# Output product begun inside the attention loop, norms applied after it, half of the gate product beside transposes

## The chip, the cores and the metric

One core of a Trainium2 chip runs the whole kernel in one launch. The time is the device time of one execution in microseconds (us), the median of the runs shown. Engines: PE (TensorE, matrix products), PEld (its weight loads), DVE (VectorE), ACT (ScalarE), POOL (GpSimd), SP (SyncE, which only issues DMAs here). PSUM has 8 banks of 128 x 512 f32.

## What is computed

256 tokens of width 2048 pass through two blocks, batch 1, all f32. The change lies in the first one:

```
h = rms_norm(x);  proj = h @ w_in                # c_q 512, c_kv 256, k_rope 64, x_rec 1024, y_gate 1024
attn = mla(c_q, c_kv, k_rope)                    # 8 heads, q/k of 128+64 (rope), v of 128, causal, blocks of 128
rec  = gelu(y_gate) * scan(a, b(x_rec))          # gated linear recurrence over the 256 tokens, 1024 features
mixed = concat(rms_norm(attn) * g_a, rms_norm(rec) * g_r)
x = x + mixed @ w_out
x = x + peer_ffn(rms_norm(x))                    # 8 heads x top 16 of 16384 experts, rows gathered for every token
```

`peer_ffn` gathers, for each token, 128 rows of `peer_u` (dot products with the token) and 128 rows of `peer_v` (weighted sum), 8 KB each. The second block takes this x and a context of 256 tokens. Its first layer projects both to queries, keys, values and gates, runs a chunked recurrence and an output product; its second layer is a gated spatial mixer. Both are modulated by `cond @ ada_w + ada_b`, where `ada_w` is 96 slabs of 1 MB (48 for each layer), which the kernel reads one by one from its first microsecond on.

## The kernel before

Every engine has one instruction stream written out by hand, with semaphores between them. Activations lie as [feature, token] for products by feature and [token, feature] for products by token. A `Plan` lays down in advance which of the 8 PSUM banks each product takes (in turn: unit number modulo 8), and in which order SP loads weight slabs of 1 MB into a ring of 4 slots. A slot is loaded again when its release semaphore is reached, in the order of the plan: a load that waits holds back all loads behind it.

The stages of the first block in PE's order: `xT` transposes; the input product in parts (`in_q`, `in_kv`, `in_x`); `uq` and `ukv` (queries, keys, values); `gates` (8 small products, 256 wide, for the recurrence); `in_y` (the gate product, 2 chunks of 4 slots); `qkT` (16 units of transposes of q and k, for which PE waits on `qk_ready`, DVE's norms and rotations); the attention loop; the output product `w_out` (4 chunks of 512 features, 4 slots each, L905 and L906); and the query product `pq` of peer_ffn with the scores `psc` per head.

**The attention loop** has 18 steps, software-pipelined over 16 units (8 heads x 2 token blocks): in step s PE does the score of unit s (L873, L874), the transposes of the probabilities of unit s-1 (L882) and the value product of unit s-2 (L889). DVE moves the scores to SBUF with the mask (L1936), takes the maximum (L1940) and the reciprocal of the sum (L1945); ACT does the exponential with the sum (L1297), evacuates the transposed probabilities (L1303) and the output with the reciprocal as factor (L1311). In step 11 the squares of the recurrent part are summed over features by 8 products with a matrix of ones (`rec_ss`, L897); ACT and DVE make a factor per token, and DVE applies it with the gain to `MIX[0:8]` (L1958).

**After the loop** DVE sums the squares of the attention output, makes the norm and scales; PE transposes it in 16 tiles (`att_turn`, before slot 1 of `w_out` chunk 0); ACT and DVE evacuate it with the gain to `MIX[8:16]`. Then `w_out` goes on. DVE adds each of its 8 units to x (L1987). `f_turn(c)` transposes chunk c of the new x for the query product.

**Slabs of ada_w.** DVE takes the dot products of each slab with one or two condition rows (L1744, `ada_dots`); `ADA_FIRST` says how many slabs at which point of DVE's stream, 48 in all before the gathers begin: among them 8 ahead of the norms and rotations (key `ukv`), 21 in `w_out`, and 3 just ahead of the first top-16 search (key `pq`). POOL issues these 48 loads. The other 48 come through SP's ring in the second block (`ADA_AT`: how many behind each slot of a chunk).

**The recurrence.** POOL multiplies the input gate by the conv output (L619, wait `ix_ready`); DVE makes the factors (L1903, L1904, L1907), scans (L1910) and then evacuates the rope part of `qkT`; POOL multiplies the scan by the gelu of the gate (L623) and squares it (L625).

**Scores.** ACT evacuates the query of head h (L1363), then the scores of head h-1 (L1355). DVE's search of head 0 (L2015 on) waits for the scores of head 0, and POOL's first gather (L646) for that search.

## Time and profile before

| | us |
|---|---|
| median of 3 runs (lowest, highest) | 2701.57 (2695.4, 2702.32) |
| profiled execution, its own time | 2707.62 |
| span of that execution | 2705.8 |
| PE busy | 1948.8 (72%) |
| DVE busy | 1973.8 (73%) |
| ACT busy | 567.8 (21%) |
| POOL busy | 1051.9 (39%) |
| attention loop, first score to first w_out product | 235.24 to 287.08 |
| w_out until PE turns to the query product | 287.08 to 402.77 |
| first gather issued | 442.37 |
| second block's first transpose | 1812.93 |

The busy shares are averages over stages with different limits. The span has four parts: the dense first block to about 403 us, the query product and the start of the gathers, the gathers to 1812 us, and the second block.

### The profile page before, as it was taken

The numbers are of one execution on the slowest core, as the hardware profiler recorded it, in microseconds if no ns is written. First come the engines' busy times: TensorE is split into PE (matmuls) and PEld (weight loads), VectorE is DVE, ScalarE is ACT, GpSimd is POOL, SyncE is SP. The second block draws the span as 40 slices with busy tenths as digits, with TensorE's granted clock in tenths as the row PEclk, the third lists the DMA queues.
The fourth block names the chain that finished last, engine by engine and source line by source line (L and its number), as shares of the span: only waits on it lengthen the run. The fifth ranks groups of instructions, "written<-read, shape, count | busy, mean of one in ns | idle before, by whom it ended". The sixth has DMA issues, their size and how long they took to land.

```text
span 2705.8 us, 20658 instructions
## 1 busy us (share of the span) xinstructions
PE 1948.8 (72%) x7632; PEld 1336.7 (49%) x7632; DVE 1973.8 (73%) x2459; ACT 567.8 (21%) x829; POOL 1051.9 (39%) x648
## 2 busy tenths in 40 slices
PE   8999999799003777777777000019999999899997
PEld 5876448647001222222222000019888887788885
DVE  6885886886997667544444999998855689777666
ACT  3043110100000000010000000013443343544343
POOL 0011002363687555545545788850065650000000
PEclk9997999899556999999999555559999999999998
DMA  9671787999999999999999999977853459677552
GB/s 374 251 292 64 293 333 282 404 371 421 416 422 422 421 421 422 422 422 421 422 422 422 421 422 422 421 315 283 323 190 125 170 180 359 262 295 286 207 200 100
DMA packets 123508, 887.60 MB, mean 328 GB/s; under 512 B 13840, under 2 KB 14352, under 8 KB 16528
## 3 DMA queue, kind: packets, MB, share of 16 engines
q0 software_dynamic: 80640, 587.24, 52.6%
q1 hardware_dynamic: 39024, 276.58, 27.5%
q10 hardware_dynamic: 3744, 22.47, 2.1%
q8 instruction: 61, 1.00, 0.1%
q14 instruction: 39, 0.32, 0.0%
HBM read 884.13 MB, written 2.10 MB: 328 GB/s over the span
## 4 chain that ended last, share of the span: by engine, by line
PE 38%; DMA 26%; POOL 16%; DVE 15%; issue 4%; ACT 2%; ACTq 0%; DVEq 0%; SPq 0%
PE psum L778 22%; DMA W<-in_peer_v,W 15%; POOL W L646 9%; POOL early_rows L646 6%; PE psum L710 6%; DMA W<-in_peer_u,W 5%; PE psum L975 3%; PE psum L734 2%; DVE split L1758 2%; DMA early_rows<-in_peer_v,W 2%; DMA early_rows<-in_peer_u,W 1%; DVE early_rows L2085 1%; DVE W L2085 1%; PE psum L926 1%; DMA ring<-in_w_even 1%
## 5 line engine op out<-in xcount | busy, mean ns | idle before, releaser
L778 PE MATMUL psum<-split,hi 128*128 128x512 f32 x1664 | 516.0, 391 | 5.4 <-DVE split L1758 4.0
L2085 DVE CUSTOM_DVE_ANT_0 W<-W,XN 128x2048 f32<-128x2048 f32 x147 | 334.2, 2292 | 207.4 <-DMA W<-in_peer_u,W 206.6
L1209 ACT ACTIVATE split<-ring 128x1024 fp32r<-128x1024 f32 x272 | 283.0, 1057 | 405.0 <-PE psum L778 299.1
L975 PE MATMUL psum<-early_rows,HT 128*128 128x512 f32 x408 | 189.1, 607 | 246.9 <-ACT HT L1415 181.0
L975 PE MATMUL psum<-W,HT 128*128 128x512 f32 x616 | 284.1, 604 | 99.2 <-DMA W<-in_peer_v,W 99.2
L2085 DVE CUSTOM_DVE_ANT_0 early_rows<-early_rows,XN 128x2048 f32<-128x2048 f32 x109 | 247.7, 2291 | 140.8 <-DMA early_rows<-in_peer_u,W 139.5
L778 PEld LDWEIGHTS psum<-split,hi 128*128 128x128 f32 x1664 | 312.2, 188 | 72.1 <-issue 6.1
L1758 DVE TENSOR_TENSOR split<-ring,split 128x1024 fp32r<-128x1024 f32 x208 | 250.3, 1227 | 130.2 <-ACT split L1209 129.2
L646 POOL DMA_INDIRECT W<-in_peer_v,W x153 | 280.5, 1833 | 163.3 <-PE psum L975 129.9
L646 POOL DMA_INDIRECT W<-in_peer_u,W x147 | 207.2, 1410 | 143.6 <-DVE W L2085 58.2
L975 PEld LDWEIGHTS psum<-early_rows,HT 128*128 128x128 f32 x408 | 74.1, 191 | 361.5 <-issue 260.9
L975 PEld LDWEIGHTS psum<-W,HT 128*128 128x128 f32 x616 | 111.5, 190 | 271.7 <-ACT HT L1415 148.8
L672 POOL TENSOR_TENSOR split<-ring,split 128x1024 fp32r<-128x1024 f32 x64 | 159.8, 2519 | 213.8 <-ACT split L1209 213.8
L988 PE MATMUL psum<-cst,X 128*128 128x128 f32 x32 | 5.1, 333 | 322.0 <-DVE X L2169 322.0
L646 POOL DMA_INDIRECT early_rows<-in_peer_v,W x103 | 184.0, 1786 | 116.8 <-PE psum L975 97.4
L646 POOL DMA_INDIRECT early_rows<-in_peer_u,W x109 | 157.6, 1446 | 121.7 <-DVE W L2085 93.7
L2163 DVE SCALAR_TENSOR_TENSOR X<-W,X 128x2048 f32<-128x2048 f32 x75 | 176.4, 2352 | 10.5 <-DMA W<-in_peer_v,W 1.2
L1415 ACT ACTIVATE HT<-cst,W 128x128 f32<-128x128 f32 x128 | 51.1, 401 | 566.6 <-PE psum L975 566.6
L734 PE MATMUL psum<-HT,ring 128*128 128x256 f32 x768 | 166.5, 379 | 0.0
L988 PEld LDWEIGHTS psum<-cst,X 128*128 128x128 f32 x32 | 4.8, 179 | 322.9 <-DVE X L2169 322.9
L734 PEld LDWEIGHTS psum<-HT,ring 128*128 128x128 f32 x768 | 145.8, 190 | 20.3 <-issue 0.4
L778 PE MATMUL psum<-split,lo_odd 128*128 128x512 f32 x384 | 149.5, 389 | 0.0
(366 smaller groups left out, 3126.9 us busy)
## 6 DMA issues: line engine op xcount, KB each, us to landing
ring<-in_ada SPq DMA_DIRECT2D x48, 1024.0 KB, 6.1
ring<-in_odd SPq DMA_DIRECT2D x48, 1024.0 KB, 5.2
XN<-in_ada POOLq DMA_DIRECT2D x21, 1024.0 KB, 8.3
early_rows<-in_ada POOLq DMA_DIRECT2D x16, 1024.0 KB, 8.1
ring<-in_w_out SPq DMA_DIRECT2D x16, 1024.0 KB, 7.6
ring<-in_pq SPq DMA_DIRECT2D x16, 1024.0 KB, 9.3
ring<-in_c_v SPq DMA_DIRECT2D x16, 1024.0 KB, 7.7
ring<-in_c_k SPq DMA_DIRECT2D x16, 1024.0 KB, 7.9
```

The costliest lines, as they stand in the source:

```text
L646: nc.gpsimd.indirect_dma_start(row, None, t["peer_" + table], bass.IndirectOffsetOnAxis(ap=EIDX[:, c:c + 1], axis=0),).then_inc(full, 16)
L672: nc.gpsimd.tensor_tensor(split[:, to + 1024:to + 2048], ring[:, at:at + 1024], split[:, to:to + 1024], ALU.subtract).then_inc(sem("lo_poo ...
L710: m = nc.tensor.matmul(o[tt][:, 0:width], lhs[:, k, tt * P:(tt + 1) * P], sl[:, kk * width:(kk + 1) * width], start=(k == 0), stop=(k == s ...
L734: m = nc.tensor.matmul(o[a][:, S * b:S * b + S], sl[:, kk * 512 + m4 * P:kk * 512 + m4 * P + P], rhs[:, k, :], start=(k == 0 and b == 0), ...
L778: m = nc.tensor.matmul(dst, lhs, rhs, start=(k == 0 and b == 0 and not (features and i % 2)), stop=(k == KD - 1 and b == 2 and not (featur ...
L926: m = nc.tensor.matmul(o[:, S * b:S * b + S], sl[:, k * P:(k + 1) * P], ht[:, k, :], start=(k == 0 and b == 0), stop=(k == KD - 1 and b == 1))
L975: m = nc.tensor.matmul(o[c], DIAG[j % DIAGS], row[:, 512 * c:512 * c + 512], start=(j == 0), stop=(j == P - 1))
L1209: A(split[:, 2048 * (n % PIECES):2048 * (n % PIECES) + 1024], ring[:, at:at + 1024], ACT.Copy)\
L1415: A(DIAG[j % DIAGS], IDENT, ACT.Copy, scale=PACT[:, j:j + 1]).then_inc(sem("diag_ready"), 1)
L1758: TT_(split[:, to + 1024:to + 2048], ring[:, at:at + 1024], split[:, to:to + 1024], ALU.subtract)\
L2085: V.tensor_tensor_reduce(out=row, in0=row, in1=xn3[:, tt, :], scale=1.0, scalar=0.0, op0=ALU.mult, op1=ALU.add, accum_out=PACT[:, c:c + 1])\
L2163: STT(x3[:, 1, :], row, PACT[:, P + j:P + j + 1], x3[:, 1, :], ALU.mult, ALU.add)\
```

## The change

- `in_y` chunk 1 is cut into 16 parts of 4 products. 8 parts follow chunk 0; one part follows the transposes of each head in `qkT`. Its gelu comes after `qkT` on ACT. The two banks that it fills are taken out of the turn meanwhile.
- `w_out` chunk 0 has separate accumulators for the recurrent features (`w_out_r`, slots 0 and 1) and the attention features (`w_out_a`, slots 2 and 3), and so have the other chunks. Slot 0 of chunk 0 is multiplied in steps 1 and 2 of the attention loop and slot 1 in steps 8 to 15. Slots 2 and 3 follow the loop.
- The norms of both groups become factors per token, applied when DVE adds the units of `w_out` to x: 16 additions with a factor (`out_add`) in place of 8 plain ones. The sums of squares come from 32 products with one column of ones (`mix_squares`), between slots 2 and 3 of chunk 0; `rec_ss`, `att_turn`, `ao_squares` and the scaling go.
- The value product is by feature: V is the stationary operand, its result is the transposed output, which DVE writes with the gain to MIX; ACT takes its square. The reciprocal of the softmax sum goes into a diagonal matrix (`DIAG_P`, one DVE instruction per unit), and the transposes of the probabilities become products with it. The loop has 19 steps, with lags 2 and 3 for 1 and 2.
- The squares of q are taken by ACT (16 instructions behind the evacuations of `ukv`) and no more by DVE. The product of input gate and conv output, and that of scan and gelu (in two halves), go from POOL to DVE. DVE scans a head's 256 columns and evacuates a head of `qkT` in turn.
- Slabs: of the 8 ahead of the norms 1 stays, 3 go between the two token blocks, 4 before the scans. The 3 ahead of the first search go into SP's ring, one each in `l_q` chunk 0, `l_v` chunk 0 and `l_v` chunk 1.
- ACT evacuates the scores of head h right behind the query of head h.

The diff, cut:

```diff
 
-ADA_FIRST = {"in": 8, "in_x0": 4, "in_x1": 2, "conv": 2, "ukv": 8, "w_out0": 5, "w_out1": 5, "w_out2": 5, "w_out3": 6,
-             "pq": 3}
+ADA_FIRST = {"in": 8, "in_x0": 4, "in_x1": 2, "conv": 2, "rope0": 1, "rope1": 3, "rope2": 4,
...
 ADA_AT = {}
-ADA_AT["l_q", 0] = (0, 0, 0, 1)
-for _step in (("l_q", 1), ("l_k", 0), ("l_k", 1), ("l_v", 0), ("l_v", 1)):
+ADA_AT["l_q", 0] = (0, 0, 1, 1)
+for _step in (("l_q", 1), ("l_k", 0), ("l_k", 1)):
     ADA_AT[_step] = (1, 1, 1, 0)
+ADA_AT["l_v", 0] = ADA_AT["l_v", 1] = (1, 1, 1, 1)
 ADA_AT["l_g", 0] = (4,)
...
+    y_late, out_early = [("in_y", 2), ("in_y", 3)], [("w_out_r", 0), ("w_out_r", 1)]
+    p.keep(y_late)
     p.units("qkT", 16)
-    for step in range(2 * NH + 2):
-        for name, lag in (("score", 0), ("probT", 1), ("pv", 2)):
+    for key in out_early:
+        p.place(key)
+    p.keep(out_early)
+    p.give_back(y_late)
+    for step in range(2 * NH + 3):
+        for name, lag in (("score", 0), ("probT", 2), ("pv", 3)):
             if 0 <= step - lag < 2 * NH:
-                p.unit[name, step - lag] = len(p.unit)
-        if step == REC_STEP:
-            p.units("rec_ss", 1)
...
+            def y_part(k):
+
+                s, kk = k // 4, k % 4
+                n = plan.slot["in_y", 1, s]
+                if kk == 0:
+                    slot_of("in_y", 1, s)
+                sl = ring[:, 2048 * (n % RING):2048 * (n % RING) + 2048]
+                for m4 in range(4):
+                    a, b = m4 // 2, m4 % 2
+                    m = nc.tensor.matmul(y_units[a][:, S * b:S * b + S], sl[:, kk * 512 + m4 * P:kk * 512 + m4 * P + P],
+                                         ht[:, k, :], start=(k == 0 and b == 0), stop=(k == KD - 1 and b == 1))
+                    if k == KD - 1 and b == 1:
+                        close(m, ("in_y", 2 + a))
+                if kk == 3 and s < 3:
+                    m.then_inc(sem("slot_used"), 1)
+
+            for k in range(8):
+                y_part(k)
             pe.wait_ge(sem("qk_ready"), TT)
             for h in range(NH):
                 for i, (n, qs, ks) in enumerate(((DN, lambda tt: qr4[:, tt, h, 0:DN], lambda tt: kv4[:, tt, h, 0:DN]),
...
                     close(m, ("qkT", 2 * h + i))
-            pe.wait_ge(sem("qkT_act"), NH)
-            pe.wait_ge(sem("qkT_dve"), NH)
...
+                    pe.wait_ge(sem("mix_rec"), 4)
+                    slot_of("w_out", 0, 0)
+                    out_part(0, 0, range(0, 2))
+                if step == 2:
+                    out_part(0, 0, range(2, 4))
+                if 8 <= step < 16:
+                    n = step - 8
+                    if n == 0:
+                        pe.wait_ge(sem("mix_rec"), 8)
+                        slot_of("w_out", 0, 1)
+                    out_part(0, 1, [n // 2], [n % 2])
+                i = step - 2
                 if 0 <= i < 2 * NH:
-                    pe.wait_ge(sem("prob_ready"), i + 1)
+                    pe.wait_ge(sem("att_diag"), i + 1)
                     o = open_unit(("probT", i))
                     for kt in range(i % 2 + 1):
-                        m = nc.tensor.transpose(o[:, kt * P:(kt + 1) * P], PR[:, i % 2, kt * P:(kt + 1) * P], IDENT)
+                        m = nc.tensor.matmul(o[:, kt * P:(kt + 1) * P], PR[:, i % 2, kt * P:(kt + 1) * P],
+                                             DIAG_P[:, i % 2, :], start=True, stop=True)
...
                 if 0 <= i < 2 * NH:
                     pe.wait_ge(sem("probT_ready"), i + 1)
                     o = open_unit(("pv", i))
                     for kt in range(i % 2 + 1):
-                        m = nc.tensor.matmul(o[:, 0:P], PT[:, i % 2, kt * P:(kt + 1) * P], kv4[:, kt, i // 2, DN:2 * DN],
+                        m = nc.tensor.matmul(o[:, 0:P], kv4[:, kt, i // 2, DN:2 * DN], PT[:, i % 2, kt * P:(kt + 1) * P],
                                              start=(kt == 0), stop=(kt == i % 2))
...
-                transposes("attT", 8, lambda k, tt: AO[:, tt, k * P:(k + 1) * P])
-
-            pe.wait_ge(sem("mix_rec"), 8)
-            token_chunk("w_out", 0, MIX, before={1: att_turn, 2: lambda: pe.wait_ge(sem("mix_att"), 4)})
+
+
+            def mix_squares():
+                pe.wait_ge(sem("rec_sq"), 1)
+                pe.wait_ge(sem("att_sq"), 2 * NH)
+                o = open_unit(("ss", 0))
+                sq3 = GA.rearrange("p (j s) -> p j s", j=8)
+                for half, sq in enumerate((SQA, sq3)):
+                    for tt in range(TT):
+                        at = 2 * half + tt
+                        for j in range(8):
+                            m = nc.tensor.matmul(o[:, at:at + 1], sq[:, j, tt * P:(tt + 1) * P], ONES[:, 0:1],
+                                                 start=(at == 0 and j == 0), stop=(at == 3 and j == 7))
+                close(m, ("ss", 0))
+
             def f_turn(c):
                 def turn():
...
 
+            out_open("w_out_a", 0)
+            slot_of("w_out", 0, 2)
+            for kk in range(4):
+                pe.wait_ge(sem("mix_att"), 2 * kk + 2)
+                out_part(0, 2, [kk])
+            mix_squares()
...
                 give(m, ("ukv", i))
+
+                if i % 2:
+                    tt = i // 4
+                    if tt:
+                        act.wait_ge(sem("q_ss"), NH)
+                    for h in range(2 * (i % 4) - 2, 2 * (i % 4) + 2):
+                        A(SQQ[:, h, :], qr4[:, tt, h, :], ACT.Square, accum_out=st(120 + 8 * tt + h))\
...
-            gelus(1)
-            for i in (2, 3):
-                gave(act, ("in_y", i))
+            gave(act, ("in_y", 1))
             act.sem_inc(sem("yg_ready"), 1)
 
+
+            used = plan.release[plan.slot["in_y", 1, 1]][0][1]
+            act.wait_ge(sem("slot_used"), used)
             for h in range(NH):
                 wait_unit(act, ("qkT", 2 * h))
...
+            def att_square(i):
                 wait_unit(act, ("pv", i))
-                m = A(AO[:, i % 2, (i // 2) * P:(i // 2 + 1) * P], bank(("pv", i))[:, 0:P], ACT.Copy, scale=st(80 + i))
-                give(m, ("pv", i))
...
-                if h:
-                    scores_evac(h - 1)
-            scores_evac(PH - 1)
+                scores_evac(h)
...
 
-            ada_dots(ADA_FIRST["ukv"])
+            ada_dots(ADA_FIRST["rope0"])
...
                 dve.sem_inc(sem("qk_ready"), 1)
-
+                if tt == 0:
+                    ada_dots(ADA_FIRST["rope1"])
...
             dve.wait_ge(sem("tanh_ready"), 8)
             dve.wait_ge(sem("decay_sq"), 1)
             seq(STT(TMP, TMP, 1.0, RR, ALU.add, ALU.mult))
             TS(TMP, TMP, 1.0e-30, None, ALU.max).then_inc(sem("mult_sq"), 1)
+            ada_dots(ADA_FIRST["rope2"])
             dve.wait_ge(sem("mult_ready"), 1)
-            dve.wait_ge(sem("ix_ready"), 1)
             seq(TT_(TMP, TMP, II, ALU.mult))
...
+            def rec_product(half):
+                a = slice(1024 * half, 1024 * half + 1024)
+                dve.wait_ge(sem("yg_ready"), half + 1)
+                seq(TT_(II[:, a], XC[:, a], YG[:, a], ALU.mult))
+                dve.sem_inc(sem("rec_out"), 1)
+
+            def rec_gain(half):
+                for j in range(4 * half, 4 * half + 4):
+                    TS(MIX[:, j, :], II[:, S * j:S * j + S], column("rec_g", j), None, ALU.mult).then_inc(sem("mix_rec"), 1)
+
+            for h in range(NH):
+                a = slice(S * h, S * h + S)
                 seq(V.tensor_tensor_scan(XC[:, a], GA[:, a], TMP[:, a], 0.0, ALU.mult, ALU.add))
...
+                if step == 1:
+                    rec_product(1)
+                    rec_gain(1)
+
...
+                    TS(DIAG_P[:, i % 2, :], IDENT, st(80 + i), None, ALU.mult).then_inc(sem("att_diag"), 1)
...
+                    m = TS(MIX[:, 8 + h, tt * P:(tt + 1) * P], bank(("pv", i))[:, 0:P], column("attn_g", h), None, ALU.mult)
...
+            def out_add(name, c, at):
+
+                for tt in range(TT):
+                    i = 2 * c + tt
+                    wait_unit(dve, (name, i))
+                    dst = x3[:, tt, 512 * c:512 * c + 512]
+                    m = STT(dst, bank((name, i)), st(at + tt), dst, ALU.mult, ALU.add)
+                    give(m, (name, i))
+                    gave(dve, (name, i))
+                    if name == "w_out_a":
...
+            for c in range(4):
+                ada_dots(2)
+                if c == 0:
+                    wait_unit(dve, ("ss", 0))
+                    m = V.tensor_copy(st(16, 4), bank(("ss", 0))[:, 0:4])
+                    give(m, ("ss", 0))
+                    gave(dve, ("ss", 0))
+                    rstd(st(12, 4), st(16, 4), ATT, EPS)
+                out_add("w_out_r", c, 14)
+                ada_dots(ADA_FIRST[f"w_out{c}"] - 2)
+                if c:
+                    evac_T("fT", ht, scale=lambda k: column("ffn_g", k), units=(2 * c - 1,))
+                out_add("w_out_a", c, 12)
```

## Rows read from the trace of the kernel before

**Rows 1.** One line of the page's costliest groups: busy, mean ns | idle before, releaser

```profile
L2085 DVE CUSTOM_DVE_ANT_0 W<-W,XN 128x2048 f32<-128x2048 f32 x147 | 334.2, 2292 | 207.4 <-DMA W<-in_peer_u,W 206.6
```

**Rows 2.** Windows, one core: window, length, busy time (instructions) per engine, PEclk, DMA share, GB/s

```profile
245.00:250.00 5.00, 5.00 (x17) 3.25 (x17) 1.68 (x7) 1.98 (x8) 0.00 (x0) 0.50 0.00 0
272.00:275.00 3.00, 3.00 (x18) 2.10 (x18) 2.24 (x10) 1.79 (x5) 0.00 (x0) 1.00 0.00 0
431.00:443.00 12.00, 12.00 (x62) 10.66 (x61) 8.01 (x35) 1.44 (x3) 0.63 (x1) 1.00 0.41 129
1000.00:1200.00 200.00, 148.59 (x323) 58.20 (x322) 116.39 (x163) 17.65 (x42) 102.55 (x80) 0.99 1.01 421
```

**Rows 3.** PE timeline before attention: start, duration, line, instructions [idle before <-releaser]

```profile
164.35 55.42 PE L734 MATMUL psum<-HT,ring 128*128 128x256 f32 x256
228.05 1.05 PE L863 MATMUL psum<-cst,W 128*64 128x128 f32 x6 [4.35 <-DVE XN L1916]
```

**Rows 4.** PE timeline in the attention loop: pair starts at either clock, and w_out's start

```profile
244.75 0.63 PE L873 MATMUL psum<-HT 128*128 128x128 f32 x2
...
250.21 0.63 PE L873 MATMUL psum<-HT 128*128 128x128 f32 x2
...
271.48 0.38 PE L873 MATMUL psum<-HT 128*128 128x128 f32 x2
...
274.47 0.39 PE L873 MATMUL psum<-HT 128*128 128x128 f32 x2
...
287.08 8.48 PE L710 MATMUL psum<-ring,W 128*128 128x512 f32 x16
```

**Rows 5.** PE timeline of the output product and the first query head

```profile
339.22 27.63 PE L710 MATMUL psum<-ring,W 128*128 128x512 f32 x64
...
407.95 1.04 PE L914 MATMUL psum<-cst,X 128*128 128x128 f32 x8
408.82 10.53 PE L926 MATMUL psum<-HT,ring 128*128 128x256 f32 x48
419.19 1.05 PE L937 MATMUL psum<-W 128*128 128x128 f32 x8
```

**Rows 6.** The chain that ended last: start, length, what

```profile
153.22 9.97 DMA XN<-in_ada
```

**Rows 7.** DVE timeline of the norms and rotations

```profile
176.49 6.07 DVE L1883 TENSOR_TENSOR W<-W 128x1536 f32<-128x1536 f32 x1
...
197.04 1.76 DVE L1883 TENSOR_TENSOR W<-W 128x1536 f32<-128x1536 f32 x1
...
213.36 2.29 DVE L1903 SCALAR_TENSOR_TENSOR W<-W 128x2048 f32<-128x2048 f32 x1 [0.22 <-DVE W L1898]
```

**Rows 8.** DVE groups of the attention stretch, and three rows of its timeline after

```profile
L1936 DVE SCALAR_TENSOR_TENSOR W<-psum,stat,cst 128x128 f32<-128x128 f32 (+1 forms) x16 | 6.7, 417 | 25.7 <-PE psum L874 25.6
L1940 DVE TENSOR_REDUCE stat<-W 128x1 f32<-128x128 f32 (+1 forms) x16 | 5.6, 353 | 0.6
...
298.99 2.35 DVE L1744 CUSTOM_DVE_ANT_0 early_rows<-early_rows,col 128x2048 f32<-128x2048 f32 x1 [0.37 <-DVE W L1971]
...
402.97 0.69 DVE L1987 TENSOR_TENSOR X<-psum,X 128x512 f32<-128x512 f32 x1 [0.17 <-PE psum L710]
...
433.65 0.49 DVE L2015 MAX8 W<-W 128x8 f32<-128x128 f32 x2 [5.03 <-ACT W L1355]
```

**Rows 9.** ACT timeline: a value product's evacuation, and the first scores

```profile
156.78 0.60 ACT L1251 ACTIVATE X<-psum 128x512 f32<-128x512 f32 x1 [1.98 <-PE psum L710]
...
417.66 0.60 ACT L1363 ACTIVATE W<-psum 128x512 f32<-128x512 f32 x1 [8.09 <-PE psum L926]
...
433.14 0.84 ACT L1355 ACTIVATE W<-psum,stat 128x256 f32<-128x256 f32 x2 [0.18 <-ACT W L1363]
```

**Rows 10.** SP's queue of DMA issues in the value chunks of the second block

```profile
1915.06 0.33 SPq L584 DMA_DIRECT2D ring<-in_c_v  x1
...
1957.26 0.33 SPq L584 DMA_DIRECT2D ring<-in_c_v  x1
```

238 lines of the change are left out of this document (118 added, 120 removed).

## The prediction

> **What bounds the kernel now.** I read the page's slices first, then the chain that ended last, then the windows and timelines of the stretch that the change touches. From the first gather to the second block the kernel is bound by DMA: in the middle of the gathers the DMA share is 1.01 and the rate 421 GB/s [rows 2] (the window of 200 us), and DVE's dot products of u rows sat 206.6 us waiting for rows [rows 1]. Nothing in the change alters the bytes gathered. So the first part counts only by when it lets the gathers start, and by how well the DMA engines are used until then. The first part is bound by PE for most of its length: `in_y` runs 55.42 us without a break [rows 3], the output product 27.63 us for every 64 instructions [rows 5]. Between these two lies the stretch that the change aims at: `qkT`, where PE waits 4.35 us for DVE [rows 3], and the attention loop, where a pair of steps takes 5.46 us at the lower clock (244.75 to 250.21) and 2.99 us at the full one (271.48 to 274.47) [rows 4]. The granted clock there is 0.50 although PE is busy 5.0 of 5 us [rows 2]. DVE has much room in it: its mask instructions waited 25.6 us for scores [rows 8].
>
> **PE's new path to the output product.** `in_y` still costs 55.4 us from 164.35 [rows 3], now with the transposes of `qkT` inside: 64 of 0.11 us (eight take 0.87 us from start to start, 407.95 to 408.82 [rows 5]), 7.0 us. If nothing stalls, the loop starts at 164.4 + 55.4 + 7.0 = 226.8.
>
> Three waits could break that. (1) PE waits for `qk_ready` at 164.4 + 55.4 x 3/4 = 205.9. DVE begins its norms when ACT has evacuated `ukv`, 158.3 (the last pair starts at 156.78 [rows 9]), and no more at 176.5 behind 8 slabs, one of which landed 9.97 us after its issue [rows 6]. One token block took 213.36 - 197.04 = 16.3 us [rows 7]; without q's square and its reduction, 1.76 us each, it takes 12.8. Two blocks and three slabs of 2 dots or one, here single ones of 2.35 us [rows 8], end at 158.3 + 25.6 + 7.1 = 191: 15 us of room. ACT's 16 squares are narrower than the 256-wide score copies (0.42 us each [rows 9]) but also read an accumulator; at 0.42 to 0.6 us, four fit in the 1.98 us that ACT idles before each pair of `ukv` [rows 9], so they cost nothing, and 2 us if late, inside the same room. (2) The first rope copy of `qkT`: DVE does two 2048-wide products at 2.29 us [rows 7], one scaling of 1.2, four dots (9.4) and one more product: 191 + 17.5 = 208.5, plus what the last slab is late. Its place comes free only after the first of those four dots (about 199) and a load lands 5 to 10 us later, so DVE starts its scans between 208.5 and 213.5. PE can run three heads ahead (6 banks), until about 213.6. So the cost is 0 to 4 us, taken as 1. (3) In the loop's step 1 PE waits for `mix_rec` 4, about 1 us after the last copy, with the probabilities of all units queued behind it: 1 us, up to 5 if (2) is late.
>
> **The loop.** Eight pairs at 3.0 us [rows 4] are 24.0. The 24 transposes of probabilities become f32 products with twice the instructions: 24 x 0.11 = 2.6. Half of `w_out` chunk 0, 32 instructions at 27.63/64 = 0.43 us [rows 5], is 13.8; it only moves, from behind the loop. DVE per step: mask 0.42, maximum 0.35 [rows 8], reciprocal, diagonal and evacuation, each no larger than these: some 1.8 us with handshakes, so a pair takes 3.6 where PE alone would take 3.3. That costs 0.5 us in the unfilled steps; the filled ones (5.1 us a pair on PE) hide it. The last value products are a chain of three engines: 1.5 us. With the waits (2) and (3) the loop ends at L = 226.8 + 24.0 + 2.6 + 13.8 + 0.5 + 1.5 + 2 = 271. In the old kernel `w_out` began at 287.08 [rows 4] with nothing done.
>
> **The output product.** PE: second half of chunk 0 13.8; `mix_squares`, 64 instructions of one column. No row shows a product of one column with full weights; the transposes load as much: 64 x 0.11 = 7.0 us, bounded by 0 and by twice that at the lower clock. Then three chunks 82.9, three `f_turn` 2.6, and the 24 instructions of the query product ahead of `f_turn(3)`, 5.2. `f_turn(3)` starts at L + 111.5 = 382.5, against 407.95 [rows 5]: 25.5 us earlier. DVE beside it: 37 dots at 2.35 [rows 8] are 87; 16 additions of 0.69 [rows 8] and a handshake 12.5; norms and evacuations 6; and it begins only when x is reloaded, 5 to 10 us after L. That ends at L + 112: DVE is as late as PE. Its time is an upper one, since the dots overlap a little, but here the gain could lose 5 us. The old attention norm, its 16 transposes and `rec_ss` are gone from both; that is in the sum already, as what no longer stands between.
>
> **The first search.** In the old kernel the scores of head 0 were computed at 419.19 [rows 5] and evacuated at 433.14, behind the query of head 1 [rows 9]; the search started at 433.65 after 5.03 us of idleness [rows 8]. Now it can start about 1.9 us after 419.19, as that row shifts: 12 us sooner still. The three dots that go, 7 us of DVE, lay in this idle time and are worth nothing beyond it. But the gathers are bound by DMA bytes: 12 us of earlier issue is worth only what the DMA engines idled there, 1 - 0.41 of 12 us = 7 (window 431 to 443 [rows 2]), less the time until the first rows flow. I take 5, with bounds 2 and 12.
>
> **The second block.** Three slabs more go through SP's ring. In the value chunks 14 loads took 1957.26 - 1915.06 = 42.2 us, 3.25 each [rows 10], and the chain there runs through the ring. The one in `l_v` chunk 0 costs 3.25. The one in `l_q` chunk 0 lies beside products of PE, the last in `l_v` chunk 1 behind that chunk's own loads: 0 to 3.25 each. I take 5 us, bounds 2 and 10. Behind SP's waits stand only ring loads.
>
> **POOL and ACT queues.** POOL loses two 2048-wide products. One ran beside DVE's square of q, which took 6.07 us against 1.76 for its twin [rows 7]; that is gone. The one left falls beside DVE's first steps of the loop and can slow them by 4 us, under PE's 6.9 us of filler. The slab loads behind POOL's wait for `rec_out` come at 231, as before.
>
> **Sum.** 25.5 + 5 - 5 = 25.5 us. The profiled execution took 2707.6 (span 2705.8); it would take 2682. It stands 6 us over the median 2701.6, so on the median's scale 2676.
>
> **The clock.** The loop's 43 us are reckoned at the full clock, and this is the largest bet. For it: PE comes from 62 us of products without a long pause; the 3 us at 272 to 275 held 1.00; and the gathers' products, busy 148.6 of 200 us, held 0.99 [rows 2]. Against it: the old loop stayed at 0.50 for 30 us while recorded as busy throughout [rows 2, 4]. The Trainium skill, "TensorE: Matmul & The Clock Gate", Part 1, says that sustained activity lifts the throttle; by that alone the old loop would have warmed, and the row says it did not. The same page, Part 4 (PE-mode transpose), says transposes do not count as activity like other products; that would make the new loop, where the probabilities' transposes became products, warmer than the old. No row here separates the two.
>
> **Rivals.**
> A, the forecast: 2676, its own range 2665 to 2688; chance 0.53.
> B, part of the loop is cold: the unfilled steps (3 to 7, 16 to 18, four pairs) go at 5.46 + 0.6 in place of 3.6: +10 us, 2686; chance 0.15.
> C, slower: PE pauses at the rope copies (wait 2), the clock falls, and as in the old loop does not return before `w_out`. Then the loop is 8 x 5.46 + 5.1 + 27.5 = 76 us in place of 43, +33; with 4 us of wait and 4 us for a cold `w_out` start and `mix_squares`, 2676 + 41 = 2717. It decides once the loop costs over 34 us more than reckoned. Chance 0.05.
> D, DVE's slabs bind the output product and the ring's turn costs its upper bound: 5 + 5 + 2 for the evacuations: 2688; chance 0.12. For it: DVE's sum equals PE's.
> E, more is gained: the search's lead counts in full (12 in place of 5) because the later DMA gaps close too, and the moved slabs cost 2: 2666; chance 0.10.
> F, the change doesn't do what it says: the gathers' end is held by something other than their start, and only the first block is shorter: 2700; against it, the DMA share of 1.01 from there on. Chance 0.05.
>
> **How the numbers follow.** Predicted 2676. The range 2659 to 2699 leaves out C and a part of F. A measurement of this kernel can tell about 0.3%, 8 us, from no change: faster means below 2693.5. Of A, B, D and E nearly all lies below: 0.87. Within: F and the edge of B and D, 0.08. Slower: C, 0.05.
>
> **What would show it.** No idle of PE over 2 us between `in_y` and the loop's start at 227; granted clock 1.00 in the loop; its pairs 3.6 us unfilled and 5.1 filled; `w_out`'s second half at 271; 64 instructions of `mix_squares` in 7 us; `f_turn(3)` at 382; first gather at 405, that is 37 us earlier; the second block's first transpose some 30 us earlier; its value chunks 5 us longer. I am wrong if the loop's pairs take 5.5 us, if DVE is still in its slabs when PE has waited for `f_turn(3)`, or if the gathers end less than 20 us earlier.

## The result, and the profile after

The changed kernel took 2688.7 us (median of 5 runs, 2683.7 to 2694.9), the kernel before 2702.3 us in the same comparison (2695.4 to 2708.8): a ratio of 0.9949, with a 95% interval of 0.9933 to 0.9965. It is faster (the whole interval lies below 1), by 13.6 us where I had forecast 25.5. On the scale of the profiled executions the sum had said 2682 against 2707.6; the profiled execution after took 2689.7 (span 2687.8), a gain of 17.9.

| step, us from the start | before | forecast | after |
|---|---|---|---|
| attention loop starts | 235.24 | 226.8 | 226.61 |
| loop ends, rest of w_out starts | 287.08 | 271 | 274.87 |
| f_turn(3) | 407.95 | 382.5 | 393.07 |
| first gather | 442.37 | 405 | 414.70 |
| second block's first transpose | 1812.93 | about 1782 | 1789.72 |
| span | 2705.8 | 2680 | 2687.8 |

The timeline of PE in the changed kernel (start, duration, line, instructions; in brackets the idle time before, with what ended it), where [rows 3 to 5] stood before:

```profile
205.79 0.38 PE L916 MATMUL psum<-cst,W 128*128 128x128 f32 x2
...
226.61 0.38 PE L952 MATMUL psum<-W,HT 128*128 128x128 f32 x2
...
242.62 0.39 PE L952 MATMUL psum<-W,HT 128*128 128x128 f32 x2
...
247.83 0.39 PE L952 MATMUL psum<-W,HT 128*128 128x128 f32 x2
...
253.57 0.39 PE L952 MATMUL psum<-W,HT 128*128 128x128 f32 x2
...
258.78 0.39 PE L952 MATMUL psum<-W,HT 128*128 128x128 f32 x2
...
274.87 7.71 PE L930 MATMUL psum<-ring,W 128*128 128x512 f32 x16
282.42 9.96 PE L995 MATMUL psum<-cst,W 128*128 128x1 f32 x64
292.23 29.93 PE L930 MATMUL psum<-ring,W 128*128 128x512 f32 x64
...
351.21 27.63 PE L930 MATMUL psum<-ring,W 128*128 128x512 f32 x64
...
391.24 1.99 PE L1035 MATMUL psum<-HT,ring 128*128 128x256 f32 x8 [1.20 <-ACTq L1278]
393.07 1.04 PE L1007 MATMUL psum<-cst,X 128*128 128x128 f32 x8
```

`qkT` starts at 205.79 with the parts of `in_y` between its transposes, nothing waits, and the loop starts where the sum had it. In the loop a pair of steps takes 5.2 us whether it has no filler (242.62 to 247.83) or has it (253.57 to 258.78): this unfilled pair, the last before the filler, is 1.6 us longer than forecast (the one ahead of it, from 238.54, took 4.08). Behind the loop the same 16 instructions take 7.71 us that take 7.03 at the full clock, `mix_squares` takes 9.96, and the 64 instructions after it take 29.93 against 27.63. The clock has its own view (windows; the fields are those of [rows 2]; PEclk is the third from the right):

```profile
250.00:260.00 10.00, 9.93 (x47) 6.32 (x46) 5.87 (x20) 3.75 (x15) 0.00 (x0) 1.00 0.01 2
...
273.00:275.00 2.00, 1.91 (x9) 1.61 (x9) 0.35 (x1) 0.66 (x2) 0.00 (x0) 0.50 1.04 438
278.00:282.00 4.00, 4.00 (x11) 1.72 (x10) 0.00 (x0) 0.00 (x0) 0.00 (x0) 1.00 0.90 340
282.00:285.00 3.00, 3.00 (x26) 2.76 (x25) 0.00 (x0) 0.00 (x0) 0.00 (x0) 1.00 1.01 423
285.00:288.00 3.00, 3.00 (x23) 3.00 (x22) 2.63 (x3) 0.00 (x0) 0.00 (x0) 0.74 1.02 431
288.00:291.00 3.00, 3.00 (x16) 3.00 (x16) 3.00 (x3) 0.00 (x0) 0.53 (x1) 0.50 0.91 385
...
403.00:416.00 13.00, 13.00 (x66) 11.54 (x65) 8.01 (x35) 1.22 (x3) 1.00 (x1) 1.00 0.65 230
```

The loop runs at 1.00, which was the largest bet (the old one at 0.50 [rows 2]). At its end, where the last value products wait for other engines, the clock falls to 0.50, recovers, and falls a second time inside `mix_squares`, some 4 us after its start, and stays low behind it. The waits of the loop, and those behind it up to the gathers (engine, tile and line that waited <- what it waited for: us in all, times, longest):

```profile
ACT W L1417 <- DVE stat L2054: 17.0, 12, 1.6
DVE W L2071 <- ACT W L1430: 10.1, 12, 1.0
...
DVE early_rows L1850 <- DMA X<-in_x: 9.6, 1, 9.6
```

In the loop VectorE waits 12 times for the square (L1430) that ScalarE takes of a value product, before it may evacuate the same product (L2071); ScalarE's exponential (L1417) in turn waits for VectorE's maximum (L2054), and the square stands behind it in ScalarE's queue. That is a ring of two queues, not a bound of PE. Behind the loop VectorE waits 9.6 us for x to be reloaded, and then works through the slabs until the last addition; PE waits 1.20 us at 391.24 for the copy of a tile that it had turned at 378.68. VectorE's last addition, ScalarE behind it, and VectorE's search:

```profile
387.82 1.65 DVE L2085 SCALAR_TENSOR_TENSOR X<-psum,stat,X 128x512 f32<-128x512 f32 x2
...
388.66 0.63 ACT L1450 ACTIVATE W<-X 128x512 f32<-128x512 f32 x1 [22.60 <-DVEq L2089]
...
390.18 0.96 ACT L1273 ACTIVATE HT<-psum,col 128x256 f32<-128x256 f32 x2
...
405.98 0.49 DVE L2127 MAX8 W<-W 128x8 f32<-128x128 f32 x2 [5.80 <-ACT W L1463]
```

```profile
414.70 1.00 POOL L680 DMA_INDIRECT W<-in_peer_u,W  x1 [40.06 <-DVEq L2179]
```

The copy (L1273) doesn't read what VectorE's last addition writes. It stands in ScalarE's queue behind the squares of the new x (L1450), and those waited 22.60 us for that addition. So VectorE's lateness reaches PE through the order of ScalarE's queue, 1.8 us after the addition has ended (389.47 to 391.24), and then PE has 8 more instructions of the query product to do before `f_turn(3)`.

The search starts at 405.98 (433.65 before [rows 8]) and the first gather is issued at 414.70, 27.7 us earlier than before: 14.9 from `f_turn(3)`, 12.8 from the earlier evacuation of the scores. The second block starts 23.2 us earlier and the span ends 18.0 earlier.

### The profile page after: what moved, and what is told of

The parts are those of the page before. It is cut to its first block, busy times and chain, and to the rows that moved or that the text cites. A ratio compares the mean times of both kernels' runs of the same rounds, so it can differ in the third digit from the quotient of the medians.

```text
span 2687.8 us, 20829 instructions
## 1 busy us (share of the span) xinstructions
PE 1945.1 (72%) x7688; PEld 1336.5 (50%) x7688; DVE 1978.4 (74%) x2460; ACT 567.1 (21%) x854; POOL 1042.9 (39%) x643
## 4 chain that ended last, share of the span: by engine, by line
PE 39%; DMA 25%; POOL 17%; DVE 13%; issue 4%; ACT 2%; ACTq 0%; DVEq 0%; SPq 0%
PE psum L812 22%; DMA W<-in_peer_v,W 15%; POOL W L680 10%; POOL early_rows L680 7%; DMA W<-in_peer_u,W 5%; PE psum L768 3%; PE psum L744 3%; PE psum L1084 3%; PE psum L930 2%; DMA early_rows<-in_peer_u,W 2%; DVE split L1864 2%; DMA ring<-in_w_even 1%; PE psum L900 1%; DVE early_rows L2197 1%; DVE W L2197 1%
## 5 line engine op out<-in xcount | busy, mean ns | idle before, releaser
L768 PE MATMUL psum<-HT,ring 128*128 128x256 f32 x640 | 138.9, 379 | 0.0
L768 PEld LDWEIGHTS psum<-HT,ring 128*128 128x128 f32 x640 | 121.4, 190 | 17.0 <-issue 0.4
```

The lines of the kernel that those rows point to most:

```text
L768: m = nc.tensor.matmul(o[a][:, S * b:S * b + S], sl[:, kk * 512 + m4 * P:kk * 512 + m4 * P + P], rhs[:, k, :], start=(k == 0 and b == 0), ...
```

## The experiments

Each kernel is the changed one with the edit shown. Milestones are of the profiled execution of each, medians and ratios (to the kernel before, timed beside it) of 5 to 12 runs; f_turn(3) is where PE turns the last tiles of x1, x2T the second block's first transpose.

| kernel | f_turn(3) | first gather | x2T | median us | ratio [95%] |
|---|---|---|---|---|---|
| changed kernel | 393.07 | 414.70 | 1789.72 | 2688.7 | 0.9949 [0.9933, 0.9965] |
| x_evac4 | 393.28 | 414.92 | 1789.55 | 2687.0 | 0.9952 [0.9940, 0.9964] |
| x_spread | 396.56 | 418.43 | 1792.45 | 2691.7 | 0.9969 [0.9957, 0.9981] |
| x_slabs | 393.40 | 422.83 | 1795.16 | 2690.5 | 0.9967 [0.9955, 0.9980] |
| x_lag | 392.89 | 427.40 | 1797.08 | 2697.2 | 0.9987 [0.9976, 0.9998] |
| x_waitx | 391.74 | 413.37 | 1787.81 | 2685.6 | 0.9942 [0.9923, 0.9960] |
| x_front | 387.58 | 410.49 | 1785.88 | 2684.2 | 0.9942 [0.9921, 0.9962] |
| x_ywhole | 404.95 | 426.59 | 1801.80 | 2700.6 | 0.9997 [0.9984, 1.0009] |
| x_nofill | 399.21 | 420.85 | 1795.99 | 2694.2 | 0.9978 [0.9964, 0.9992] |
| x_best | 396.52 | 418.08 | 1791.85 | 2682.1 | 0.9928 [0.9907, 0.9950] |
| x_evacx | 386.61 | 408.24 | 1783.71 | 2682.6 | 0.9932 [0.9914, 0.9949] |
| x_ptrans | 393.64 | 415.28 | 1789.96 | 2687.3 (1 run) | none |
| x_final | 383.64 | 405.20 | 1779.31 | 2678.9 | 0.9923 [0.9906, 0.9941] |

The intervals are 3 to 6 us wide on each side, so differences of 2 or 3 us between kernels are read from the milestones, which agree within 0.5 us at f_turn(3) where nothing ahead of them differs (x_lag, x_slabs and the changed kernel: 392.89 to 393.40) and within 0.9 us at the loop's start (226.48 to 227.31, all but x_ywhole).

**x_evac4: the ring of two queues in the loop.** VectorE's evacuation of a value product moves one step back in its own queue.

```diff
-            for step in range(2 * NH + 3):
+            for step in range(2 * NH + 4):
...
-                i = step - 3
+                i = step - 4
                 if 0 <= i < 2 * NH:
                     h, tt = i // 2, i % 2
                     dve.wait_ge(sem("att_sq"), i + 1)
```

> The changed kernel, with VectorE's evacuation of a value product into MIX one step later in its queue (lag 4 in place of 3), so that its next mask no longer stands behind ScalarE's square of the same unit. Theory (the attention loop is a chain VectorE mask, maximum, ScalarE exponential, copy, square, VectorE evacuation, mask again, 2.6 us a step, whatever TensorE does): the unfilled pairs (from 242.6) fall from 5.2 us to about 4, the filled ones stay at 5.1 by TensorE, the loop is 4 to 6 us shorter, total 2684. Rival 1 (TensorE bounds the loop, it is recorded as busy): pairs stay 5.2, total 2689, no gain. Rival 2 (the loop gets shorter but VectorE's slabs behind it, done at 389 us, hold the output product): loop 5 us shorter, f_turn(3) at most 3 us earlier, total 2687.

PE, x_evac4:

```profile
242.69 0.39 PE L952 MATMUL psum<-W,HT 128*128 128x128 f32 x2
...
246.44 0.39 PE L952 MATMUL psum<-W,HT 128*128 128x128 f32 x2
...
270.25 7.03 PE L930 MATMUL psum<-ring,W 128*128 128x512 f32 x16
277.12 10.63 PE L995 MATMUL psum<-cst,W 128*128 128x1 f32 x64
287.61 29.23 PE L930 MATMUL psum<-ring,W 128*128 128x512 f32 x64
...
389.90 3.54 PE L1035 MATMUL psum<-HT,ring 128*128 128x256 f32 x8 [5.18 <-ACTq L1278]
```

An unfilled pair takes 3.75 us (242.69 to 246.44), near the forecast's 3.6, and the rest of w_out starts at 270.25 in place of 274.87: the ring had cost 4.6 us, some 1.5 in the unfilled pair, 0.8 in the four filled ones (5.14 us each here) and 2.4 behind the last score, where the clock fell in the changed kernel and did not here. Nothing of it arrived. PE waits 5.18 us ahead of f_turn(3), and the 8 instructions behind that pause take 3.54 us where 1.99 do without it. So rival 2 of the expectation holds, with even less gain than it gave: the loop was bound by the chain of VectorE and ScalarE, and the stretch behind it by VectorE, whose lateness ScalarE's queue passes on. VectorE's last addition ends at 388.13, 1.3 us earlier than in the changed kernel, and f_turn(3) starts 5.2 us after that end (3.6 in the changed kernel): ScalarE's squares of x and the copy behind them come in between, then the 8 instructions at the low clock. With the copy ahead of the squares in ScalarE's queue f_turn(3) could have followed at about 388 (an estimate from these rows); no run tests it. VectorE waits 12.9 us for x in place of 9.6, until 284.03 (285.37 in the changed kernel): the reload starts 4.6 us earlier and lands 1.3 earlier.

**x_spread: what mix_squares costs, and the clock.** The 32 products leave their place behind the loop; the plan gives `ss` a bank of its own for the loop.

```diff
+                if 4 <= step < 8:
...
+                    for n in range(4 * (step - 4), 4 * (step - 4) + 4):
+                        square_sum(1, n // 8, n % 8)
+                i = step - 4
+                if 0 <= i < 2 * NH:
+                    pe.wait_ge(sem("att_sq"), i + 1)
+                    square_sum(0, i % 2, i // 2)
...
-            mix_squares()
```

> The changed kernel, with the 32 products of mix_squares taken from their place between the parts of w_out and spread over the attention loop (recurrent ones in steps 4 to 7, one attention one per step from step 4). Theory (at its place mix_squares cost 9.96 us and let the clock fall for some 3 us more of the products behind it; in the loop TensorE has room because the loop runs at the pace of other engines): loop 0 to 3 us longer, f_turn(3) 9 to 13 us earlier (about 382), total 2679. Rival 1 (VectorE's slabs beside the output product, done at about 389, bind next): f_turn(3) only 4 us earlier, total 2685. Rival 2 (the loop is bound by TensorE, so the products cost there what they cost behind it): loop 10 us longer, only the clock's 3 us are won, total 2686.

PE, x_spread:

```profile
277.26 7.11 PE L930 MATMUL psum<-ring,W 128*128 128x512 f32 x16
...
284.36 27.71 PE L930 MATMUL psum<-ring,W 128*128 128x512 f32 x64
...
392.98 3.78 PE L1044 MATMUL psum<-HT,ring 128*128 128x256 f32 x8 [11.10 <-ACTq L1287]
```

The loop is 2.4 us longer, the 64 instructions behind it take 27.71 us, near the full clock's 27.63, and PE gets so far ahead of VectorE that it waits 11.10 us. f_turn(3) came 3.5 us later: 1.7 because VectorE's last addition did (389.56 for 387.82), and 1.8 because the 8 instructions behind the pause took 3.78 us for 1.99. The theory was right about PE and wrong about the total; rival 1, VectorE, bound, and harder than it said, since 5.4 us lie here too between the end of its last addition (391.21) and f_turn(3). The 7.0 us of the forecast for `mix_squares` were the price at the full clock: 34 of its 64 instructions took 3.85 us in x_final, 0.11 each. The other 3.0 us of its 9.96 are the clock, with 2.3 behind it and 0.7 ahead of it, from the loop's end: 6 us in all. In this kernel the same products, one to five in a step, did not let the clock fall.

**x_waitx and x_front: what binds behind the loop.** VectorE waited for x ahead of two slabs that don't read x.

```diff
-            for tt in range(TT):
-                dve.wait_ge(sem(f"x_loaded{tt}"), 32)
...
                 ada_dots(2)
                 if c == 0:
+                    for tt in range(TT):
+                        dve.wait_ge(sem(f"x_loaded{tt}"), 32)
                     wait_unit(dve, ("ss", 0))
```

x_waitx is this alone, x_front this with the edits of x_evac4 and x_spread.

> The changed kernel, with VectorE's wait for the reload of x (9.6 us of idleness at 285.37) moved behind the first two slabs of w_out, which don't need x. Theory (VectorE and TensorE were equally late at f_turn(3), so relief of VectorE alone is worth only the 1.2 us that TensorE waited there): VectorE reaches the last addition 9 us earlier, f_turn(3) 1.2 us earlier (391.9), total 2687.5. Rival (VectorE's lateness held more than that wait shows, such as the query product's evacuation behind it): f_turn(3) 4 us or more earlier, total 2684.

> Three edits together: the evacuation one step later, mix_squares spread over the attention loop, and VectorE's wait for x behind the first two slabs. Alone the first two moved f_turn(3) by +0.2 and +3.5 us, with TensorE waiting there 5.2 and 11.1 us. Theory (TensorE's gain was real and was lost to VectorE's slabs, which start with the wait for x): f_turn(3) at 380 to 384 in place of 393.07, first gather as much earlier, total 2679. Rival 1 (the slabs' loads, at 8.5 us each through places that VectorE frees, set VectorE's pace, not the wait for x): f_turn(3) no earlier than 389, total 2685. Rival 2 (an earlier search finds the DMA engines taken by reloads, so that the gathers end no earlier than x_lag's price of 0.6 us per us says): f_turn(3) at 382, total 2682.

Alone it moved f_turn(3) by 1.3 us, the wait of PE at 391.24, and the total by 3 us by the medians, within their error. VectorE was hardly relieved: in place of 9.6 us for x it now waits 7.3 us for the sums of `mix_squares`, and its last addition comes 1.9 us earlier (385.90). PE sets the pace from there. The forecast's two sums (L + 111.5 and L + 112) had the two engines equally late; measured without its wait PE would have been at f_turn(3) at about 391.9, 2.4 us behind the end of VectorE's last addition. In x_front the three edits together gave 5.5 us at f_turn(3), 387.58, between theory (380 to 384) and rival 1. The timeline of VectorE shows why, and PE's that it still waits:

```profile
277.54 2.35 DVE L1859 CUSTOM_DVE_ANT_0 early_rows<-early_rows,col 128x2048 f32<-128x2048 f32 x1 [0.26 <-DVE W L2080]
...
380.58 1.65 DVE L2091 SCALAR_TENSOR_TENSOR X<-psum,stat,X 128x512 f32<-128x512 f32 x2
```

```profile
384.00 3.78 PE L1044 MATMUL psum<-HT,ring 128*128 128x256 f32 x8 [4.76 <-ACTq L1287]
```

From 277.54 to the end of the last addition at 382.2 VectorE has no pause over 0.6 us: 104.7 us of work from the end of the loop, which itself ended late (276.56, x_evac4's at 270.25): with the ring open PE bounds the filled pairs, and the squares in them count. The other part is ScalarE's order: its copy began at 382.94, behind the squares of x, PE went on at 384.00 at the low clock, and f_turn(3) came 5.4 us after VectorE's last addition had ended. Without that delay it would have stood at about 382, inside the theory's range (again an estimate, not tested).

**x_nofill: is the filler free?** The second half of w_out's recurrent part of chunk 0 goes behind the loop.

```diff
-                if 8 <= step < 16:
-                    n = step - 8
-                    if n == 0:
-                        pe.wait_ge(sem("mix_rec"), 8)
-                        slot_of("w_out", 0, 1)
-                    out_part(0, 1, [n // 2], [n % 2])
...
+            pe.wait_ge(sem("mix_rec"), 8)
+            slot_of("w_out", 0, 1)
+            out_part(0, 1)
             out_open("w_out_a", 0)
```

> The changed kernel, with the second half of w_out's recurrent part of chunk 0 (16 instructions, 6.9 us) taken out of steps 8 to 15 of the attention loop and put behind it. Theory (the loop is bound by the chain through VectorE and ScalarE): pairs stay 5.2 us, the loop ends where it did, the 6.9 us come on top, f_turn(3) 5.7 us later (TensorE's wait of 1.2 goes), total 2694. Rival 1 (TensorE bounds the filled pairs): the loop is 5 to 7 us shorter, total 2689. Rival 2 (the filler is what keeps the clock up): granted clock 0.50 from step 8, loop 3 us longer or more, total 2699.

```profile
275.39 14.79 PE L930 MATMUL psum<-ring,W 128*128 128x512 f32 x32
```

The loop ended at 275.39 without the filler and at 274.87 with it, having started 0.65 later, its pairs at 5.2 us throughout; f_turn(3) came 6.1 us later. The theory holds: the loop's length is the chain's, and 6.9 us of products in steps 8 to 15 cost next to nothing there (48.26 us of loop with them, 48.13 without). The clock stayed at 1.00 without them.

**x_ywhole: is the interleaving of in_y free?** All parts of in_y ahead of qkT.

```diff
-            for k in range(8):
+            for k in range(16):
                 y_part(k)
...
-                y_part(8 + h)
```

> The changed kernel, with all 16 parts of in_y ahead of qkT, so that its 64 transposes stand in one run, as in the kernel before. Theory (the interleaving hides VectorE's eight rope copies and scans, 1.74 us a head): VectorE reaches its first mask some 9 us later (236 in place of 227.45), the loop ends 7 to 9 us later, clock 1.00 throughout because TensorE makes no pause of over 2 us, total 2697. Rival 1 (64 transposes in one run let the clock fall, as it was 0.59 behind them in the kernel before): granted clock 0.50 in the loop, pairs over 5.5 us, total over 2710. Rival 2 (TensorE is three heads ahead, so only 3 us are lost): total 2692.

f_turn(3) came 11.9 us later, and the total is that of the kernel before (ratio 0.9997). VectorE reached its first mask at 236.23 in place of 227.45, 8.8 us later, as the theory said; but the clock fell too, against the theory. Windows of x_ywhole at the loop's start and once more in its unfilled steps:

```profile
229.00:232.00 3.00, 0.47 (x4) 0.38 (x2) 2.64 (x5) 2.84 (x4) 0.00 (x0) 0.93 0.00 0
232.00:235.00 3.00, 2.79 (x7) 1.62 (x7) 2.72 (x6) 0.81 (x1) 0.00 (x0) 0.50 0.00 0
235.00:238.00 3.00, 2.34 (x4) 0.84 (x3) 2.78 (x10) 0.71 (x3) 0.00 (x0) 0.50 0.00 0
238.00:241.00 3.00, 3.00 (x5) 1.21 (x4) 2.85 (x2) 0.38 (x2) 1.98 (x1) 0.50 0.00 0
...
253.00:256.00 3.00, 1.88 (x11) 1.37 (x10) 1.77 (x6) 1.15 (x4) 0.00 (x0) 0.91 0.00 0
256.00:259.00 3.00, 3.00 (x9) 1.70 (x8) 1.77 (x7) 0.93 (x4) 0.00 (x0) 0.50 0.00 0
```

PE was busy 0.47 of 3 us there, waiting for rope copies, and went on at 0.50 until about 242. The clock was at 1.00 behind the transposes (226 to 229) and fell after PE's pauses, so rival 1's cause, the run of transposes, isn't what the windows show. It fell again at about 255.5, behind a pause of 1.06 us, and was low for some 7 us; the same pause at the same place left the changed kernel at 1.00. With the interleaving taken out, the whole gain of 13.6 us but 1.7 is gone, in two ways: VectorE's scans and copies no longer lie beside products (8.8 us), and PE pauses and loses the clock (the other 3). The costs of single parts taken out don't add up to 13.6 (11.9 here, 8.5 in x_lag, 5.5 in x_nofill, by the medians), since the change also has parts that cost time.

**x_ptrans: products or transposes.** The probabilities are turned by the identity, and the division by the softmax sums is missing from the output.

```diff
-                        m = nc.tensor.matmul(o[:, kt * P:(kt + 1) * P], PR[:, i % 2, kt * P:(kt + 1) * P],
-                                             DIAG_P[:, i % 2, :], start=True, stop=True)
+                        m = nc.tensor.transpose(o[:, kt * P:(kt + 1) * P], PR[:, i % 2, kt * P:(kt + 1) * P], IDENT)
```

> The changed kernel, with the 24 transposes of probabilities as transposes by the identity again; the division by the softmax sums is left out with it. Theory (the loop's full clock comes from the work that surrounds it without a pause, not from what form the transposes have; the loop's length comes from the chain through VectorE and ScalarE): granted clock 1.00 to 270, loop end at 274 to 275, total within 3 us of 2689. Rival (transposes lift the clock less than products): granted clock below 0.9 in the unfilled steps, loop 3 us longer or more.

```profile
244.00:247.00 3.00, 1.89 (x8) 1.24 (x9) 1.75 (x7) 1.15 (x4) 0.00 (x0) 0.89 0.00 0
247.00:250.00 3.00, 3.00 (x11) 1.90 (x10) 1.95 (x8) 1.25 (x5) 0.00 (x0) 0.50 0.00 0
...
253.00:256.00 3.00, 3.00 (x14) 1.69 (x13) 1.61 (x5) 0.67 (x3) 0.00 (x0) 0.97 0.00 0
```

At the end of the first unfilled steps, where x_nofill and the changed kernel held 1.00, the clock fell to 0.50 for some 7 us, and the loop ended at 275.85, 1.0 us later (it had started 0.5 later): the clock went as the rival said, the length as the theory. The length doesn't show what the low clock cost, since the filled pairs behind it took 4.8 us here and 5.2 in the changed kernel. The Trainium skill, "TensorE: Matmul & The Clock Gate", Part 4 (PE-mode transpose), says that transposes don't count as busy time as products do; this run agrees with it. It is one execution, with the form the number of instructions changed (24 transposes for 48), and x_ywhole's clock fell in the same steps with the transposes as products. So it is in line with the rule and does not show it.

**x_lag: the lead of the first search.**

```diff
                 act.sem_inc(sem("pq_ready"), 1)
-                scores_evac(h)
+                if h:
+                    scores_evac(h - 1)
+            scores_evac(PH - 1)
```

> The changed kernel, with the score evacuation of head h put back behind the query evacuation of head h + 1 in ScalarE's queue, as in the kernel before. Theory (the lead of 12.8 us of the first gather is worth 8 us at the end of the gathers, because the DMA engines are about 0.65 busy in that time): first gather 12 to 13 us later, x2T about 8 us later, total 2697. Rival 1 (my forecast's price): 5 us, total 2694. Rival 2 (the lead counts in full, the gathers only shift): 12.8 us, total 2701.

The first gather came 12.7 us later and x2T 7.4 us later: 0.58 us per us of lead. The theory's number holds, its reason does not: the share of 0.65 is that of 403 to 416 in the changed kernel, almost all of it ahead of the first gather at 414.70. In x_lag the DMA share was 0.34 in 414 to 427, the stretch that the lead had filled with gathers; 0.66 of 12.7 us idle there are 8.4 us, an estimate near the 7.4.

**x_slabs: the three slabs back ahead of the search.**

```diff
+             "pq": 3}
...
+ADA_PLACE += [("early", "cond")[_n % 2] for _n in range(3)]
...
-ADA_AT["l_q", 0] = (0, 0, 1, 1)
...
+ADA_AT["l_q", 0] = (0, 0, 0, 1)
...
-ADA_AT["l_v", 0] = ADA_AT["l_v", 1] = (1, 1, 1, 1)
...
             dve.wait_ge(sem("fn_ready"), 2 * TT)
+            ada_dots(ADA_FIRST["pq"])
```

> The changed kernel, with the three ada slabs put back from the second block to their old place ahead of the first search (their dot products, 3 of 2.35 us on VectorE, and their loads). Theory (the slabs cost 5.2 us in the value chunks of the second block, and ahead of the search VectorE idles 5.8 us, which hides all but 1.3 us of the 7.05): first gather 1.3 us later, second block 5 us shorter, total 2685. Rival 1 (the slabs land late, behind the reload of x, g and the query weights, and hold the search): first gather 5 us or more later, total 2689, nothing won. Rival 2 (the second block's 5 us come from elsewhere, such as the added dot products in VectorE's queue): no gain in the block, total 2690.

```profile
411.84 2.35 DVE L1853 CUSTOM_DVE_ANT_0 early_rows<-early_rows,col 128x2048 f32<-128x2048 f32 x1 [6.66 <-DMA early_rows<-in_ada]
...
422.83 1.01 POOL L683 DMA_INDIRECT W<-in_peer_u,W  x1 [19.10 <-DVEq L2183]
```

Two of the three dot products fitted into VectorE's idle time; the third waited 6.66 us for its load. The gather came 8.1 us later and x2T 5.4 later; at the transposes of x3, behind the even layer of the second block, the two kernels stood within 0.1 us (2296.81 and 2296.88), so the slabs cost 5.4 us in the second block. The theory had the block right and the search wrong, rival 1 was the case; in the total nothing is won or lost.

**x_best, x_evacx and x_final: both engines at once.** x_evacx has the edits of x_evac4 and x_waitx. x_best has them too, with the squares in steps 4 to 7 and 16 to 18, one dot product ahead of the search, and the recurrent squares added on GpSimd first:

```diff
-             "w_out0": 5, "w_out1": 5, "w_out2": 5, "w_out3": 6}
+             "w_out0": 5, "w_out1": 5, "w_out2": 5, "w_out3": 5,
+             "pq": 1}
...
             nc.gpsimd.tensor_tensor(GA, II, II, ALU.mult).then_inc(sem("rec_sq"), 1)
+            for n, half in enumerate((1024, 512, 256)):
+                pool.wait_ge(sem("rec_sq"), n + 1)
+                nc.gpsimd.tensor_tensor(GA[:, 0:half], GA[:, 0:half], GA[:, half:2 * half], ALU.add)\
+                    .then_inc(sem("rec_sq"), 1)
```

> Five edits: VectorE's evacuation one step later; its wait for x behind the first two slabs; GpSimd adds the recurrent squares over their eight blocks, so that TensorE needs 2 products for them in place of 16; the attention squares' products stand in steps 4 to 7 and 16 to 18 of the loop, where TensorE has room, and not in the filled steps; and one single slab's dot product goes behind the norm of x1, ahead of the search, where VectorE idles 5.8 us. Theory (TensorE and VectorE have to be relieved together): loop ends at 270 to 272, no low clock behind it, f_turn(3) at 378 to 381 against 393.07, search start as much earlier, total 2677. Rival 1 (VectorE's slabs still bind: its 36 dot products and additions take 102 us from the loop's end): f_turn(3) at 384, total 2682. Rival 2 (an earlier search gains only 0.6 us per us): total 2681 with f_turn(3) at 380.

> Two edits: the evacuation one step later and the wait for x behind two slabs; mix_squares stays at its place. Theory (mix_squares costs there its 10.6 us and 1.6 us of low clock behind it, spread in steps 8 to 15 of a loop that TensorE now bounds it cost 6.3): loop ends at 270.3 as in x_evac4, f_turn(3) at 386 to 387, total 2683, the same as x_front. Rival (VectorE binds both): f_turn(3) at 381, no later than x_front's slabs allow, total 2679.

x_evacx did what it should: f_turn(3) at 386.61, no wait of PE, 2682.6 us. x_best's profiled execution shows what the forecast had as rival C. VectorE, then PE, then the clock, x_best:

```profile
230.84 8.30 DVE L2040 TENSOR_SCALAR W<-W,col 128x256 f32<-128x256 f32 x4
```

```profile
239.62 0.80 PE L991 MATMUL psum<-W 128*128 128x128 f32 x2 [3.14 <-DVE W L2079]
```

```profile
238.00:241.00 3.00, 1.38 (x4) 0.93 (x4) 2.41 (x8) 0.48 (x3) 1.46 (x3) 0.59 0.88 347
250.00:260.00 10.00, 10.00 (x38) 8.03 (x37) 3.52 (x14) 3.23 (x12) 0.00 (x0) 0.50 0.01 2
```

The theory's loop end of 270 to 272 and its f_turn(3) of 378 to 381 failed in this execution. GpSimd's additions lay beside VectorE's four gains of the recurrent half (8.30 us; they took 4.52 in the changed kernel beside GpSimd's square alone, and the four of the first half, with GpSimd idle, 1.14). PE waited 3.14 us for the first diagonal, and the loop went on at 0.50 to about 269 and ended at 289.4. Yet the median is 2682, and its runs lie from 2675 to 2690, wider than the 7 us of x_evacx: the one that was profiled took 2689, and the shorter ones may be those whose clock did not fall there. The granted clock over the whole execution is in line with it (0.891 and 0.889 in the two runs of 2689 and 2690 us, 0.894 or 0.895 in the three of 2675 to 2680), but it doesn't say where the clock was low, and only one was profiled.

x_final leaves GpSimd alone and moves 15 products, into the last three steps.

```diff
+            SUMS = {16: range(0, 5), 17: range(5, 10), 18: range(10, 15)}
...
+                for i in SUMS.get(step, ()):
+                    pe.wait_ge(sem("att_sq"), i + 1)
+                    square_sum(0, i % 2, i // 2)
```

> x_evacx's two edits, and two more: 15 of the 16 attention squares' products stand in steps 16 to 18 of the loop (the recurrent ones stay behind the first four parts of w_out_a, GpSimd adds nothing), and one slab's dot product stands ahead of the search. Nothing is added to the steps in which x_best's TensorE paused. Theory (TensorE alone bounds from here: 5 us of products fewer behind the loop, 2.5 more in it, 1 us less of low clock; VectorE no longer waits 7 us for the sums): granted clock 1.00 up to the loop's end at 272 to 274, f_turn(3) at 382 to 384 against x_evacx's 386.61, total 2679. Rival 1 (a loop nearer to its limit falls into the low clock, as x_best's did): loop end past 280, total 2687. Rival 2 (the products in the last three steps cost there what they cost behind): f_turn(3) at 386, total 2682.

```profile
272.44 8.79 PE L934 MATMUL psum<-ring,W 128*128 128x512 f32 x16
281.08 3.85 PE L954 MATMUL psum<-cst,W 128*128 128x1 f32 x34
284.79 29.41 PE L934 MATMUL psum<-ring,W 128*128 128x512 f32 x64
...
383.64 1.04 PE L1016 MATMUL psum<-cst,X 128*128 128x128 f32 x8
```

The theory holds: w_out's rest starts at 272.44, with the clock at 1.00 up to there, f_turn(3) at 383.64, first gather at 405.20, 2678.9 us. x_final is 22 us faster than the kernel before (0.9923 [0.9906, 0.9941]) and 7 us (by the ratios) to 10 us (by the medians) faster than the changed one, whose interval it overlaps a little; the milestones, 9.4 us earlier at f_turn(3) and 10.4 at x2T, say the same. The low clock is not gone from it: it fell behind each of the two runs of one-column products, and the dense ones took 8.79 us where 7.03 are needed and 29.41 where 27.63 are. In x_evacx, x_final and x_waitx PE sets the pace at f_turn(3), so ScalarE's order costs nothing there.

## Why the prediction was right in sign and too high in size

The range 2659 to 2699 holds 2688.7, and the change is faster. But it came out at D's time (2688), not at A's (2676). By the steps of the prediction:

1. `in_y` and `qkT`, start of the loop: forecast 226.8, measured 226.61. Wait (1) did not arise; wait (2) was a load that VectorE waited 2.6 us for, and PE did not feel it, nor did it pause for wait (3). The 2 us that the sum had for these two did not come.
2. The clock of the loop: forecast 1.00, measured 1.00. x_ywhole and x_best show that the bet was near: they lost it behind pauses of PE of 2.5 and 3.1 us at its start.
3. The unfilled pairs: forecast 3.6 us, measured 5.2. This step failed. I had added up VectorE's instructions, 1.8 us a step, as if its queue could run ahead; the mask of the next unit stands behind the evacuation of an older one, that behind a square on ScalarE, and that behind the exponential that needs this VectorE's maximum. The sum was also uneven by itself: 0.3 us over PE's 3.3 in each of four unfilled pairs is 1.2, and it had 0.5. x_evac4 opened the ring: 3.75 us a pair, and 4.6 us in all, more than the 3.9 between 271 and 274.87. About half of that lay in the last steps, for which the sum had 1.5 us.
4. The filled pairs: forecast 5.1 by PE, measured 5.2. The price of PE was right (5.14 in x_evac4), the bound was right by chance: x_nofill's pairs take 5.2 without the filler, so it was the chain, and the two happened to be equal.
5. `mix_squares`: forecast 7.0 with bounds 0 and 14, measured 9.96. The price of an instruction was right at the full clock (0.11 us); that the low clock begins there, and lasts beyond it, was in the bound and not in the sum. The low clock, with the drop at the loop's end, cost 6 us. With 1.2 of wait that is L + 118.2 in place of L + 111.5; the rest of the sum was 0.5 too high.
6. VectorE beside w_out: forecast equal to PE (L + 112), measured L + 114.6. The term was right within 3 us, and its consequence stood only in rival D, at 0.12, as a loss of up to 5 us. What I did not draw from it: where two engines are about equally late, a later gain of one of them is worth little. What I did not see at all is ScalarE's queue, which held PE's next tile until VectorE's last addition was done; it, and the low clock behind PE's wait, are the 5.2 us by which x_evac4's f_turn(3) stands behind that addition. x_evac4 (4.6 us of PE, nothing at f_turn(3)), x_spread (PE up to 11 us ahead, a loss of 3.5) and x_waitx (one wait of VectorE gone, another in its place, 1.3) show it from both sides, x_evacx and x_final what both together give.
7. The lead of the search: forecast 5 (bounds 2 and 12), measured 7.4 of 12.7 in x_lag. The idle share of DMA in the row had given 7; what I took off for the time until the first rows flow was too much.
8. The slabs in the second block: forecast 5, measured 5.4 (x_slabs). Right.
9. The scale: the sum gave 2682 for a profiled execution, and I took 6 us off, since the profiled execution of before stood so far over its median. The one after stood 1 us over its own (2689.7 and 2688.7). Such an offset belongs to one execution and can't be carried to another kernel: 5 us of the 12.7 by which the forecast was too low are this step, and some 7.5 the steps above: 25.5 forecast and 18.0 measured in the spans, that is 10.6 less at f_turn(3), 2.4 more from the lead and 0.4 less by the slabs; 1.1 stay unassigned. The offset goes with the clock: timed beside the experiments, the kernel before took 2692.1 us with a mean granted clock of 0.894 and 2704.9 with 0.887, and its profiled execution had 0.887 (0.892 after). So the 4.4 us by which the 18.0 in the spans exceed the 13.6 in the medians may be the clock of that one execution; at which step isn't shown.

Of the rivals, A's mechanism was the right one, with 18.0 of its 25.5 us in the spans (that the median came out at D's number is chance, as D's second half did not happen and step 9 is in no rival); B's cold part of the loop did not come in the changed kernel, but in x_ptrans and x_ywhole; C's came in x_best's profiled execution with 289.4 as loop end; of D the first half, VectorE, was the case, the ring's upper bound was not. F is refuted by the table: where f_turn(3) moves, x2T moves with it, mostly in full (x_nofill 6.1 and 6.3, x_ywhole 11.9 and 12.1, x_final 9.4 and 10.4; in x_front 5.5 and 3.8).

## What to carry to other kernels

Before a stretch is priced by the instructions of its busiest engine, follow one unit around all queues: if an engine's next instruction stands behind one that needs another engine's answer to this engine's last, the stretch runs at the length of that ring, and filler on a third engine is free until it reaches it. Where two engines end a stretch together, relieve both or neither, put a wait behind the work that doesn't need it, and look through whose queue one engine's lateness reaches the other: here a copy that was ready to be made stood behind squares that were not. A gain is measured against spans of the same kind: the offset of one execution to its median can't be carried to another kernel.

## What the runs showed of the hardware

- The granted clock fell to 0.50 after pauses of PE: one of 3.14 us (x_best), one of 2.53 with shorter ones before it (x_ywhole), and those of 5 and 11 us ahead of f_turn(3) (x_evac4, x_spread, where it cost 1.6 and 1.8 us).
- It fell also with PE recorded as busy throughout: 3.3 us (x_evac4) to 4 us (the changed kernel) after the start of `mix_squares`, products of one column with full weights, and behind 15 and 34 such products in x_final. In x_spread, where they stand one to five in a step between others, it held 1.00.
- At 0.50 it stayed 7 to 31 us in the loop (x_ptrans and x_ywhole's second time 7, x_ywhole's first 10, x_best 31), and 1 to 5 us once dense products had begun (the changed kernel, to about 276 and about 297). The Trainium skill, "TensorE: Matmul & The Clock Gate", Part 1, says activity releases the throttle; x_best's loop, busy 10 of 10 us at 0.50, agrees with that only if busy time as recorded is not what is counted.
- x_nofill's loop held 1.00 with PE busy some 7.3 of 10 us, in pauses of up to 1.1 us. The same pause of 1.06 us in the same steps was followed by a fall in x_ywhole, which had been at 0.50 until some 14 us before. What makes the difference isn't shown.
- Four scalings of 128x256 on VectorE took 1.14 us with GpSimd idle, 4.52 beside a 2048-wide product on GpSimd, and 8.30 beside that and three additions (4.49 us on GpSimd).
- A us by which only the first search starts earlier was worth 0.58 us (x_lag) to 0.67 (x_slabs, 5.4 of 8.1); a us by which the whole query product and the search start earlier was worth about 1 (x_nofill, x_ywhole, x_final), 0.7 in x_front.
